# Slots of the head pieces in a two-layer attention and retention stage: three slots per head, at the ends of the panels

## What is computed

```
for l in range(2):
    h = rmsnorm(x, attn_norm[l])
    c_q, c_kv, k_rope, rq, rk, rv, rg = split(h @ w_in[l])
    a = mla_attention(c_q, c_kv, k_rope, ...)       # 8 heads, causal softmax
    r = retention(rq, rk, rv, rg, cos, sin)         # 8 heads, decay instead of softmax, group norm, gate
    x = x + concat(rmsnorm(a, beta_attn[l]), r * beta_ret[l]) @ w_o[l]
    h = rmsnorm(x, mlp_norm[l])
    x = x + square(relu(h @ w_up[l])) @ w_down[l]
out = rmsnorm(x, final_norm)
```

## Time and profile before

| | us |
|---|---|
| median of three runs | 3266.09 |
| lowest and highest | 3265.69, 3267.18 |
| the profiled execution | 3266.15 |
| its span | 3264.4 |
| TensorE matmul busy | 3239.4 (99%) |
| VectorE, ScalarE, GpSimd busy | 2141.8 (66%), 1554.7 (48%), 267.5 (8%) |

### The profile page before, as it was taken

How to read it: one execution, slowest core, us unless ns; L and a number is a source line. 1 busy time by engine, 2 the same in 40 slices (tenths; PEclk the granted TensorE clock), 3 DMA queues, 4 the chain that set the end, 5 groups by cost and what they waited for, 6 DMA issues and landing times.

```text
span 3264.4 us, 45496 instructions
## 1 busy us (share of the span) xinstructions
PE 3239.4 (99%) x17258; PEld 2795.1 (86%) x17258; DVE 2141.8 (66%) x2513; ACT 1554.7 (48%) x1815; POOL 267.5 (8%) x211
## 2 busy tenths in 40 slices
PE   8999999999999999999999999999999999999999
PEld 8999888888888888888888888888888888888887
DVE  8898665555555656555555688884656555568887
ACT  5345454344444544544434455554444544345555
POOL 6422000000000025000000000001410000000000
PEclk9999999999999999999999999999999999999999
DMA  7544565555555555455555565655545565556564
GB/s 212 166 130 156 192 206 181 193 191 185 193 193 193 171 169 182 147 186 180 181 193 192 182 205 194 201 180 173 186 144 179 193 193 186 187 186 200 194 204 155
DMA packets 249327, 598.65 MB, mean 183 GB/s; under 512 B 22296, under 2 KB 64248, under 8 KB 248184
## 3 DMA queue, kind: packets, MB, share of 16 engines
q1 hardware_dynamic: 248056, 591.17, 56.1%
q0 software_dynamic: 768, 5.24, 0.4%
q10 hardware_dynamic: 384, 0.58, 0.0%
HBM read 594.86 MB, written 2.10 MB: 183 GB/s over the span
## 4 chain that ended last, share of the span: by engine, by line
PE 96%; DVE 3%; ACT 1%; DVEq 0%; issue 0%; DMA 0%; SPq 0%; ACTq 0%
PE ps L1166 27%; PE ps L681 21%; PE ps L1421 18%; PE ps L687 11%; PE ps L1118 4%; PE ps L1069 3%; PE ps L755 2%; PE ps L763 2%; PE ps L756 2%; PE ps L1478 1%; PE ps L624 1%; PE ps L1473 1%; DVE wlo L2295 1%; PE ps L1315 0%; PE ps L1313 0%
## 5 line engine op out<-in xcount | busy, mean ns | idle before, releaser
L2295 DVE TENSOR_TENSOR wlo<-raw,whi 128x2048 fp32r<-128x2048 f32 (+1 forms) x425 | 973.2, 2290 | 587.9 <-ACT whi L1591 587.4
L1591 ACT CAST whi<-raw 128x2048 fp32r<-128x2048 f32 x425 | 805.7, 1896 | 495.1 <-PE ps L687 426.1
L681 PE MATMUL ps<-xT,whi 128*128 128x512 f32 x3072 | 733.6, 391 | 1.4 <-DVE xT L2313 1.1
L681 PEld LDWEIGHTS ps<-xT,whi 128*128 128x128 f32 x3072 | 564.6, 188 | 111.6 <-issue 1.3
L1166 PE MATMUL ps<-whi,stage 128*128 128x512 f32 x2592 | 619.8, 389 | 0.0
L1166 PEld LDWEIGHTS ps<-whi,stage 128*128 128x128 f32 x2592 | 486.2, 188 | 100.7
L1421 PE MATMUL ps<-whi,xT 128*128 128x512 f32 (+1 forms) x1792 | 444.1, 389 | 1.1 <-DVE wlo L2979 0.9
L687 PEld LDWEIGHTS ps<-xT,wlo 128*128 128x128 f32 x3072 | 393.9, 191 | 15.0
L687 PE MATMUL ps<-xT,wlo 128*128 128x256 f32 x3072 | 398.5, 283 | 0.0
L2979 DVE TENSOR_TENSOR wlo<-raw,whi 128x2048 fp32r<-128x2048 f32 (+3 forms) x126 | 276.0, 2191 | 170.5 <-ACT whi L2058 170.5
L1421 PEld LDWEIGHTS ps<-whi,xT 128*128 128x128 f32 x1792 | 326.2, 188 | 63.4 <-issue 1.7
(11 more groups left out here) (489 smaller groups left out, 2874.2 us busy)
## 6 DMA issues: line engine op xcount, KB each, us to landing
raw<-in_mlp_w SPq DMA_DIRECT2D x128, 1024.0 KB, 5.1
raw<-in_w_up SPq DMA_DIRECT2D x128, 1024.0 KB, 5.2
raw<-in_w_down SPq DMA_DIRECT2D x128, 1024.0 KB, 5.3
raw<-in_w_in SPq DMA_DIRECT2D x100, 1024.0 KB, 5.1
raw<-in_w_o SPq DMA_DIRECT2D x32, 1024.0 KB, 5.3
raw<-in_w_out SPq DMA_DIRECT2D x16, 1024.0 KB, 5.1
raw<-in_w_in SPq DMA_DIRECT2D x16, 832.0 KB, 4.4
raw<-in_w_uq SPq DMA_DIRECT2D x8, 768.0 KB, 4.3
```

Source lines behind the costliest of these rows:

```text
L681: mm(psum(bank + j), whi[:, u % 2, c:c + P], xT[:, k, :], start=k == 0, stop=False)
L1591: act.copy(whi[:, u % 2, 0:width], raw[:, u, 0:width]).then_inc(sig["hi"], 1)
L2295: tt(wlo[:, u % 2, 0:width], raw[:, u, 0:width], whi[:, u % 2, 0:width].bitcast(F32), SUB).then_inc(sig["lo"], 1)
```

## The change

Attention head m begins at slot 2 + 3m instead of 2 + 5m, retention head h at 44 + 3h instead of 45 + 3h, mix tile b at 59 + 3b instead of 57 + 3b. Scores, probabilities and values of an attention head follow 3, 6 and 9 slots later instead of 2, 5 and 7; scores and values of a retention head 3 and 6 instead of 2 and 4. All these slots are at pos 2. On TensorE the order within one slot becomes values, probabilities, scores, transposes, then mix tiles. `slot(q)` of ScalarE and VectorE has no edit but takes the new constants.

```diff
--- before.py
+++ after.py
@@ -187,19 +187,19 @@
 
 
 def mla_turn(m):
-    return 2 + 5 * m
+    return 2 + 3 * m
 
 
 def ret_turn(h):
-    return 45 + 3 * h
+    return 44 + 3 * h
 
 
 def mix_turn(b):
-    return 57 + 3 * b
-
-
-MLA_SCORES, MLA_PROBS, MLA_VALUES = 2, 5, 7
-RET_SCORES, RET_VALUES = 2, 4
+    return 59 + 3 * b
+
+
+MLA_SCORES, MLA_PROBS, MLA_VALUES = 3, 6, 9
+RET_SCORES, RET_VALUES = 3, 6
 LATENT_TURN, RET_MIX_TURN = (10, 2), (50, 2)
 FFN_TURNS = {(60, 0): 0, (60, 2): 1, (61, 1): 2, (62, 0): 3}
 
@@ -1377,21 +1377,21 @@
                     if q == mla_turn(0):
                         rope_turns()
                     for i in range(8):
-                        if q == ret_turn(i):
-                            head_transposes(i)
+                        if q == mla_turn(i) + MLA_VALUES:
+                            head_values(i)
+                        if q == ret_turn(i) + RET_VALUES:
+                            head_values(8 + i)
+                    for i in range(8):
+                        if q == mla_turn(i) + MLA_PROBS:
+                            prob_transposes(i)
                     for i in range(8):
                         if q == mla_turn(i) + MLA_SCORES:
                             head_scores(i)
                         if q == ret_turn(i) + RET_SCORES:
                             head_scores(8 + i)
                     for i in range(8):
-                        if q == mla_turn(i) + MLA_PROBS:
-                            prob_transposes(i)
-                    for i in range(8):
-                        if q == mla_turn(i) + MLA_VALUES:
-                            head_values(i)
-                        if q == ret_turn(i) + RET_VALUES:
-                            head_values(8 + i)
+                        if q == ret_turn(i):
+                            head_transposes(i)
                     for b in range(4):
                         if q == mix_turn(b):
                             mix_turned(b)
```

## The result

The changed kernel takes 3271.49 us (median of 22 runs, 3269.80 to 3273.94), the kernel before 3266.11 us (22 runs, 3265.61 to 3267.18): ratio 1.0016, 95% interval 1.0010 to 1.0022. The forecast was 3269.2 us in a range of 3265.4 to 3272.4. The time is in the range and the sign is right, but 2.3 of the 5.4 us lost weren't in the sum: the median stands 0.2 us above the forecast's own upper end (3271.3) and is in the range only by the 1.1 us added for runs that differ.

A forecast was written before the change was run, and what follows sets the result against it. It took TensorE's own matmul stream, busy throughout the heads' stage, as the bound. Stalls of 4.8 us less 1.7 us of saved interruptions gave +3.1 on 3266.15: 3269.2 us, range 3265.4 to 3272.4.

The forecast's parts named there:

- part 1: TensorE's stream in the heads' stage: 42 fewer interruptions over two layers at 0.04 us each, 1.7 us gained.
- The sign that the stage would be 0.8 us shorter up to the end of rg: Sign of being right: each layer's heads' stage, up to rg's end, shorter by 0.8 us.
- Rival D: Small groups on TensorE: interruptions are free, so no gain offsets the 4.8 us; 3270.9 us, chance 0.04.
- part 2: Attention heads at one per panel: softmax takes at most about 5.0 us, inside 6.1 us of cover; nothing priced.
- part 4: Last retention values now behind rg's end: TensorE stalls 2.4 us per layer before o0, 4.8 in two layers.
- Rival B: Ahead of o0: the stall is hidden after all and only the gain is left; 3264.5 us, chance 0.03.
- Rival A: Ahead of o0: short stall of 1.25 us per layer, VectorE's queue clear at the last values' end; 3266.9 us, chance 0.18.
- part 3: Retention transposes, mix tiles, loads, casts and low parts moved half a panel: covered in general, except at the last values; nothing.
- Rival C: Last rg panel: its low part comes late and TensorE waits in both layers; 3272.6 us and more, chance 0.11.
- The clock: Sign of being wrong: a granted clock under 1.00 behind the stall ahead of o0; no size given.

The follow-up runs named there:

- e6_cleared: Changed kernel with last values at slot 70, first retention transposes at slot 45, VectorE's low part of o0's first panel behind the last moments; 3265.09 us.
- e8_more_cuts: Kernel before, with the attention values one slot later, alone instead of with the next head's scores; 3267.01 us.
- e7_attention_only: Kernel before, with the new slots and order for the attention heads alone; retention heads and mix tiles stay; 3265.73 us.
- e2_before71: Kernel before, with the last retention head's values in slot 71, behind rg's end; 3268.80 us.
- e4_moments_first: Changed kernel, with VectorE taking the last retention head's moments ahead of its two evictions of rg; 3268.30 us.
- e1_last70: Changed kernel, with the last retention head's values back in slot 70, ahead of the last six matmuls of rg; 3267.49 us.
- e5_first45: e4_moments_first, with the first retention head's transposes at slot 45 again instead of 44; 3267.61 us.
- e3_busy: Changed kernel, with nine idle 128x128 matmuls on TensorE ahead of o0's wait for the copy; 3270.17 us.

## Why the prediction was right, and where it was short

**The interruptions (part 1)** were right in place and nearly in size. The traces have 42 groups per layer before and 21 after. They were priced at 0.04 each; e6_cleared, which has none of the waits, shows 0.66 us per layer, 0.031 each, so 1.3 us in all instead of 1.7. The sign that the stage would be 0.8 us shorter up to the end of rg did not show in the changed kernel: it is 0.25 shorter there, since 0.41 are lost at the end of rv. Rival D, that they are free, fell with e6_cleared and e8_more_cuts.

**The attention heads (part 2)** were right: nothing was priced, and e7_attention_only shows no wait.

**The last values (part 4)** were the main term, 2.4 us per layer. By the chain as worked out, the cast was to start 3.7 us behind the start of the group before (3.57 measured, 1393.46 - 1389.89), the low part to end at 7.93 (7.81) and TensorE to go on 3.14 behind the panel's end (1399.98 - 1397.11 = 2.87). Each link was right to 0.3 us, so the 2.4 was not luck. The stage holds 180.21 - 177.53 (e6_cleared, which saves as many interruptions) = 2.68 us of waits, of which 0.41 belong to the next point: 2.27. e2_before71 and e4_moments_first take the two halves apart: 1.3 for the slot, 0.9 for the evictions behind the late low part, and e1_last70 has 1.0 for that late low part without the slot. Rival B, that the stall is hidden, is refuted by the 2.04 us of idle. Rival A, the short stall, would have needed VectorE clear; it was not, and e1_last70 shows that the delayed low part would have held up the moments even in the old slot.

**The moves of half a panel (part 3)** are the step that failed: they were put at nothing. It read: casts and low parts are now queued behind the pieces of the group before, "That is covered in general, but not at one place". There was a second place, the end of rv. I had followed GpSimd's rotations to slot 44, but not ScalarE's copy and table load there, ahead of the cast of rg's first panel. It cost 0.41 us per layer, 0.8 in all, shown by e5_first45. Rival C had its finger on such a chain, at the last rg panel; no wait is seen there.

**The clock** was named only as a thing that would prove the forecast wrong, with no price. By the prediction's own list this sign of being wrong came true. It adds 1.6 us where it falls. All four profiles of the changed kernel have one fall. Without it the time would have been some 3269.9 us, 0.7 above the forecast, so the range held in spite of a cost that it had no term for.

The sum as measured, per layer: 2.27 + 0.41 - 0.66 = 2.02 against 180.21 - 178.21 = 2.00 in the second layer's stage. Two layers, 4.0, plus one fall, 1.6, make 5.6; the difference of the two spans is 5.3, as the changed execution reached its first layer 0.33 us earlier, and that of the medians 5.4. The forecast had +3.1: interruptions 0.4 too high a gain, stalls 0.3 too high, and 0.8 and 1.6 not in it.

## To carry to other kernels

When small pieces move in an engine's stream, write down for each place where they now meet what the other two engines have in their queues there, up to the next thing that the first engine waits for: casts, evictions, table loads. Look for waits in the rows of the weight loads too: a short wait may hardly show between the matmuls' records. A group that is cheap in the middle of a product is not cheap at its end, where the next product waits for the banks. Keep cover behind the last link of such a chain and give that link the first place in the second engine's queue: with the cast kept early too, that turned a loss of 2.0 us per layer into a gain of 0.66.

## What had not been expected of the hardware

An idle time of 2.03 to 2.04 us of TensorE, after more than a thousand us at full clock, was followed by a stretch of 3.4 us at 0.50 in the first layer in all four profiles, and by none in the second layer, with the same idle time. With work put into that idle time (e3_busy) there was none in either layer. Idle times of 0.68 and 1.08 us were followed by none at these places. What makes the first layer differ was not tried. Nearly the same stretches (3.4 us at 0.50) also stand in the first 31 us of some executions (e4_moments_first at 27 to 31 us, for one) and not of others: in six of the thirteen profiles. The start of the kernel, up to the first layer's rope transposes, takes 1236.0 to 1237.1 us in the runs of this study, so single executions of one kernel can be a us apart with the stage the same. These early stretches alone don't set it: it is 1236.12 to 1237.09 with one and 1236.02 to 1236.64 without.
